# Input matrices of a state-space layer: powers turned once and read back by channel group, coefficients taken from a row layout

## The chip, the cores and the metric

The kernel is one program on one core of a Trainium2 chip. The metric is the device time of one execution in microseconds (us), smaller is better. The engines named are TensorE (PE; its weight loads are listed apart as PEld), VectorE (DVE), ScalarE (ACT), GpSimd (POOL) and SyncE (SP). SP and ACT each issue transfers on a DMA queue of their own (SPq, ACTq). Engines run their own lists of instructions in order and wait for one another through semaphores.

## What is computed

Two transformer blocks run one after the other on 512 tokens of width 1024, in float32. The first block has an attention layer with its MLP and a state-space layer with its MLP; the second is a modulated block with convolution, attention and a gated FFN. The change concerns matrices that the state-space layer needs and that depend on weights only:

```python
dt = jnp.exp(log_dt)[..., None]
a_bar = jnp.exp(lam * dt)                       # complex, per direction, group and state
b_bar = ((a_bar - 1.0) / lam)[..., None] * b_mat
bu = jnp.einsum('sgh,gph->sgp', u_row, b_bar[r])
...   # h_t = a_bar * h_(t-1) + bu_t, in both directions
return jnp.einsum('sgp,ghp->sgh', states, c_mat[r]).real
```

There are 64 groups of 16 channels, 64 states and 2 directions. The kernel cuts the 512 tokens into 64 chunks of 8. For that it needs, for each group, an "input matrix" that carries the 8 tokens x 16 channels of a chunk (128 rows) to the 2 directions x 64 states (128 columns), real and imaginary: each entry is a power of `a_bar` (by token in the chunk) times a coefficient of `b_mat` (by channel) times the gain of the norm. An "output matrix" and a "lag kernel" (what a token does to the others of its chunk) are built from the same powers.

## The kernel before

All weights come as units of 128 x 1024 numbers. A unit is loaded by SP into `raw`, rounded to the matmul's format by ACT (`hi`, L1115, tile `WH`), and DVE takes the rest of it (`lo`, L1643, tile `WL`). A product of two split operands is three matmuls (L444, L445, L446). SP loads a unit into a slot of `raw` when DVE is done with the one before (`unit_ready`).

The MLP of the first layer runs as 64 steps k = 0..63, each 24 matmuls of 128x512 on PE, in two halves of 32. Steps 0 to 15 of a half are up-projection tiles: ACT evicts each with L1328 and L1330, DVE splits it with L2056 (`AH`) and L2058 (`AL`). Steps 16 to 23 and 24 to 31 are the down-projection's two column halves; after step 23 and step 31 DVE adds four tiles of PSUM to `h` (L2072). Step 32, the first of the second half, uses PSUM banks that the evictions after step 31 free (`down_add`).

Beside the steps each engine calls `beside(k)`, an order that is written out by hand: the state-space matrices are built there, in 16 blocks b of 4 groups, block b around step `TURNS[b]`:

```python
TURNS = (9, 12, 17, 20, 24, 27, 30, 32, 35, 38, 41, 44, 49, 52, 57, 60)
```

The powers come first. DVE computes them in `beside(0)` to `beside(2)` (`powers`, `input_powers`) and, in `beside(4)`, the output powers (`output_powers`: L1810, L1814, L1815, tiles `pd` and `PC`). Then for each block, with T = TURNS[b]:

- ACT, step T-4: loads the block's coefficients with the states on partitions, `bc`.
- DVE, step T-2: `input_matrix(b)`: the gain into `bc` (L1827), four products of 512 per partition (L1829), a difference and a sum (L1833, L1835), into `WIp` with states on partitions.
- DVE, step T-1: `output_matrix(b)` (four of L1845, then L1850 and L1852).
- PE, after step T: `matrices(b)`: eight 128x128 transposes of `WIp` into PSUM (L558). ACT copies them to `WIe` (L1155) and stores it to `wi_scratch` (L1157).
- PE, after step T+1: `kernels(b)`: 16 small matmuls for the lag kernels (L573); ACT evicts them and stores the output matrix and, a step later, the kernels; DVE mends the middle lag (`lag_zero`, L1859, L1862) in step T+2.

The state-space layer after the MLP loads `wi_scratch` back (SP, L389). DVE comes to a step's `beside` after its share of the step's own work, so `beside(k)` on DVE runs after PE has ended step k, while PE is in step k+1.

## Time and profile before

| | |
|---|---|
| time, median of 3 runs | 1870.07 us (1869.59 to 1875.5) |
| profiled execution: its own time / its span | 1871.1 us / 1869.3 us |
| PE busy | 1788.6 us (96%) |
| DVE busy | 1298.9 us (69%) |
| ACT busy | 780.1 us (42%) |
| mean granted TensorE clock | 0.984 of full speed |
| moved by DMA | 224.98 MB, 120 GB/s |
| the chain that ended last | PE 89%, DVE 8%, ACT 1%, issue 1% |

The span is from the first to the last instruction; the time of the execution has 1.8 us around it. The chain that ended last is followed back from the last instruction to what released each step. A share of busy time is a mean over stages with different limits, so the stage of the change has to be read by itself: the first layer's MLP lies at about 300 to 660 us of the span.

### The profile page before, as it was taken

Reading aid. Unit: us, or ns where it says so; the run is one execution under the profiler, and the core shown is the slowest. Engines: PE = TensorE matmul, PEld = TensorE weight load, DVE = VectorE, ACT = ScalarE, POOL = GpSimd, SP = SyncE. Lnnn points to the kernel's source line nnn. Section 1 sums busy time; section 2 is a strip of 40 time slices with the busy share of each in tenths; the row PEclk is TensorE's granted clock in tenths of the full one; section 3 lists DMA queues with packets and bytes.
Section 4 is the critical chain, followed back from the end, with each engine's and each line's share of the span. In section 5 each row is a group of like instructions: output and inputs, shape, how many; then the busy total and the mean of one; then the engine's idle time right before and its main releaser. Section 6 shows DMA issues by size and latency. Waiting matters only on the chain.

```text
span 1869.3 us, 25467 instructions
## 1 busy us (share of the span) xinstructions
PE 1788.6 (96%) x9314; PEld 1439.4 (77%) x9314; DVE 1298.9 (69%) x2395; ACT 780.1 (42%) x1273; POOL 48.2 (3%) x39
## 2 busy tenths in 40 slices
PE   7999999999999992999999999999999999999998
PEld 6886688888888862888888788779755778888886
DVE  4868967767886669536655686448899976677465
ACT  5237954422342372424321332244687343333211
POOL 0000000000000000000000000000043100000000
PEclk9999999999999995999999999999999999999999
DMA  7320022444554489433444676224111223223532
GB/s 212 102 90 23 1 70 97 143 148 150 172 156 153 141 254 139 149 100 136 147 146 147 202 231 226 79 68 125 35 35 46 68 80 103 98 90 101 180 102 68
DMA packets 99927, 224.98 MB, mean 120 GB/s; under 512 B 19296, under 2 KB 48608, under 8 KB 99824
## 3 DMA queue, kind: packets, MB, share of 16 engines
q1 hardware_dynamic: 53520, 166.81, 28.8%
q10 hardware_dynamic: 46304, 56.77, 9.8%
q8 instruction: 67, 1.10, 0.2%
q14 instruction: 36, 0.29, 0.1%
HBM read 202.68 MB, written 20.87 MB: 120 GB/s over the span
## 4 chain that ended last, share of the span: by engine, by line
PE 89%; DVE 8%; ACT 1%; issue 1%; ACTq 0%; DVEq 0%
PE PS L444 26%; PE PS L445 26%; PE PS L446 26%; PE PS L634 2%; DVE ST L2125 1%; PE PS L1020 1%; PE PS L659 1%; PE PS L994 1%; DVE Sst L2129 1%; DVE Sst L2132 1%; PE PS L647 1%; PE PS L1028 1%; PE PS L558 1%; PE PS L504 1%; PE PS L1021 1%; PE PS L779 1%
## 5 line engine op out<-in xcount | busy, mean ns | idle before, releaser
L1643 DVE TENSOR_TENSOR WL<-raw,WH 128x1024 fp32r<-128x1024 f32 x228 | 279.7, 1232 | 275.9 <-ACT WH L1115 266.5
L1115 ACT CAST WH<-raw 128x1024 fp32r<-128x1024 f32 x228 | 237.3, 1046 | 489.5 <-PE PS L446 410.2
L444 PE MATMUL PS<-XH,WH 128*128 128x512 f32 x928 | 366.3, 395 | 4.5 <-DVE XL L1677 4.3
L446 PE MATMUL PS<-XH,WL 128*128 128x512 f32 x928 | 362.8, 391 | 0.0
L445 PE MATMUL PS<-XL,WH 128*128 128x512 f32 x928 | 362.6, 391 | 0.0
L444 PE MATMUL PS<-WH,AH 128*128 128x512 f32 x688 | 269.6, 392 | 0.0
L446 PE MATMUL PS<-WH,AL 128*128 128x512 f32 x688 | 267.9, 389 | 0.0
L445 PE MATMUL PS<-WL,AH 128*128 128x512 f32 x688 | 267.7, 389 | 0.0
L444 PE MATMUL PS<-WH,XH 128*128 128x512 f32 (+2 forms) x512 | 197.7, 386 | 11.6 <-DVE XL L1713 10.6
L444 PEld LDWEIGHTS PS<-XH,WH 128*128 128x128 f32 x928 | 175.0, 189 | 43.1 <-DVE XL L1677 4.9
L446 PEld LDWEIGHTS PS<-XH,WL 128*128 128x128 f32 x928 | 175.0, 189 | 37.2
L445 PEld LDWEIGHTS PS<-XL,WH 128*128 128x128 f32 x928 | 175.2, 189 | 34.9
L445 PE MATMUL PS<-WL,XH 128*128 128x512 f32 (+2 forms) x512 | 195.5, 382 | 0.0
L444 PEld LDWEIGHTS PS<-WH,AH 128*128 128x128 f32 x688 | 129.1, 188 | 28.8 <-issue 2.6
L446 PEld LDWEIGHTS PS<-WH,AL 128*128 128x128 f32 x688 | 129.1, 188 | 27.2
L445 PEld LDWEIGHTS PS<-WL,AH 128*128 128x128 f32 x688 | 129.2, 188 | 26.3
L446 PE MATMUL PS<-WH,XL 128*128 128x512 f32 (+2 forms) x384 | 145.7, 380 | 0.0
L1328 ACT ACTIVATE tmp<-PS 128x512 f32<-128x512 f32 x64 | 38.3, 598 | 197.4 <-PE PS L446 197.4
L444 PEld LDWEIGHTS PS<-WH,XH 128*128 128x128 f32 x512 | 96.8, 189 | 30.9 <-issue 11.2
L445 PEld LDWEIGHTS PS<-WL,XH 128*128 128x128 f32 x512 | 96.9, 189 | 17.4 <-issue 0.2
L1608 ACT ACTIVATE F<-PS,fb,fw 128x512 f32<-128x512 f32 x44 | 34.3, 780 | 142.9 <-PE PS L446 142.9
L2056 DVE CAST AH<-tmp 128x512 fp32r<-128x512 f32 x64 | 27.2, 425 | 83.1 <-ACT tmp L1330 82.6
(369 smaller groups left out, 2465.8 us busy)
## 6 DMA issues: line engine op xcount, KB each, us to landing
raw<-units_dram SPq DMA_DIRECT2D x272, 512.0 KB, 3.3
ada_late<-ada_units_dram ACTq DMA_DIRECT2D x48, 512.0 KB, 4.3
wi_scratch<-WIe ACTq DMA_DIRECT2D x16, 512.0 KB, 2.9
ca_scratch<-CAr ACTq DMA_DIRECT2D x32, 256.0 KB, 3.5
WI<-wi_scratch SPq DMA_DIRECT2D x16, 512.0 KB, 8.8
CA<-ca_scratch SPq DMA_DIRECT2D x16, 512.0 KB, 7.0
Tm<-k_scratch SPq DMA_DIRECT2D x8, 512.0 KB, 18.4
bc<-bc_dram ACTq DMA_DIRECT2D x16, 160.0 KB, 2.2
```

The source lines that it names most:

```text
L444: pe.matmul(o, lh, rh, start=start, stop=False)
L445: pe.matmul(o, lh, rl, start=False, stop=False)
L446: return pe.matmul(o, ll, rh, start=False, stop=stop)
L504: m = pe.transpose(turned_columns(ts, k, t, bank), h[:, t, k * P:(k + 1) * P], ident[:, :])
L558: m = pe.transpose(PS[:, bank0(k) + n // 4, (n % 4) * P:(n % 4 + 1) * P], WIp[:, n % 2, n // 2].rearrange("p j h -> p (j h)"), ident[:, :])
L634: m = pe.matmul(psum(2 * (n % 2) + c), QT[r, hh, t * P:(t + 1) * P], KT[r, hh, :], start=True, stop=True)
L647: m = pe.transpose(psum(4 + i % 2)[:, kt * P:(kt + 1) * P], Am[:, i % 2, kt * P:(kt + 1) * P], ident[:, :])
L1115: nc.scalar.copy(WH[:, (u + n) % SLOTS], raw[:, s]).then_inc(hi_done, 1)
L1328: nc.scalar.activation(tmp[:, f % 2, :], psum(4 + f if layer and first and f < 2 else f % 4), ACT.Relu).then_inc(up_relu, 1)
L1608: nc.scalar.activation(F[:, half, q, :], psum(up2_bank(f, first)), ACT.Identity, scale=fw[:, bass.ds(n, 1), 1], bias=fb[:, bass.ds(n, 1)]) ...
L1643: v.tensor_tensor(WL[:, s], raw[:, (u + n) % 2], WH[:, s].bitcast(F32), ALU.subtract).then_inc(unit_ready, 1)
L2056: v.tensor_copy(AH[:, f, :], tmp[:, 2 + f % 2, :]).then_inc(up_hi, 1)
```

## The change

The input matrix is built with tokens and channels on partitions from the start, the way it is stored. The powers (`PWI`, 128 x 8 x 128) are transposed once, after step 5 (8 transposes), and written to DRAM (`p_scratch`). For each block ACT then loads `PT`, the turned powers, each row of 8 tokens repeated to 16 channels, and `BT`, coefficients from a new input `bt` whose 16 channel rows are repeated for 8 tokens. DVE multiplies `PT` by `BT` and by the gain (now a scalar per partition, `gain_t`) in eight instructions of 256 instead of four of 512, and adds and subtracts into `WIe`, which is stored at once. `matrices(b)` and its eviction are gone, `output_powers` moves from `beside(4)` to `beside(3)`, and its end is signalled to PE (`w_done`). The gain is still multiplied into `bc`, since the lag kernels use it.

```diff
+        p_dram = nc.dram_tensor("p_scratch", [CHUNK, NG, 2, P], F32).ap()
...
-                def matrices(b):
+                def powers_turned():
+
+                    pe.wait_ge(w_done, 1)
+                    for j in range(CHUNK):
+                        m = pe.transpose(PS[:, 4 + j // 4, (j % 4) * P:(j % 4 + 1) * P], PWI[:, j].rearrange("p r g -> p (r g)"), ident[:, :])
+                    m.then_inc(m_turned, 1)
...
-                    pe.wait_ge(w_done, 2 * b + 2)
+                    pe.wait_ge(ca_done, 2 * b + 2)
                     if k // 8 % 4 == 2:
                         pe.wait_ge(up_relu, 16 * (k // 32 + 1))
                     if k // 8 % 4 == 3:
                         pe.wait_ge(down_add, 8 * (k // 32) + 4)
-                    if b:
-                        pe.wait_ge(ev_wi, b)
-                    for n in range(2 * BG):
-                        m = pe.transpose(PS[:, bank0(k) + n // 4, (n % 4) * P:(n % 4 + 1) * P],
-                                         WIp[:, n % 2, n // 2].rearrange("p j h -> p (j h)"), ident[:, :])
-                    m.then_inc(m_turned, 1)
...
-                        elif k in TURNS:
-                            matrices(TURNS.index(k))
+                        elif k == 5:
+                            powers_turned()
...
-                def evict_wi(b):
-
-                    bank = 0 if TURNS[b] // 8 % 4 == 2 else 4
-                    a.wait_ge(m_turned, b + 1)
-                    if b:
-                        a.wait_ge(wi_stored, 16 * b)
-                    nc.scalar.copy(WIe[:, :], PS[:, bank:bank + 2, :].rearrange("p a n -> p (a n)")).then_inc(ev_wi, 1)
-                    a.wait_ge(ev_wi, b + 1)
-                    a.dma_start(wi_dram[b], WIe[:, :]).then_inc(wi_stored, 16)
+                def evict_powers():
+
+                    a.wait_ge(m_turned, 1)
+                    nc.scalar.copy(WIe[:, :, :, :].rearrange("p g r q -> p (g r q)"), PS[:, 4:6, :].rearrange("p a n -> p (a n)")).then_inc(ev_wi, 1)
+                    a.wait_ge(ev_wi, 1)
+                    for r in range(2):
+                        a.dma_start(p_dram[:, :, r, :].rearrange("j g q -> g j q"),
+                                    WIe[64 * r:64 * r + 64].rearrange("g a r q -> g (a r) q")).then_inc(wi_stored, 16)
+
+                def pb_load(b):
+
+                    pairs = lambda x: x[:, :, :, :].rearrange("p g r q -> p (g r q)")
+                    sh = [CHUNK, SG, 2 * BG * P]
+                    a.dma_start(pairs(PT), p_dram[:, BG * b:BG * (b + 1)].rearrange("j g r q -> j (g r q)").unsqueeze(1).to_broadcast(sh)).then_inc(pb_in, 16)
+                    a.dma_start(pairs(BT), io["bt"][b].unsqueeze(0).to_broadcast(sh)).then_inc(pb_in, 16)
+
+                def store_wi(b):
+
+                    a.wait_ge(w_done, 2 * b + 3)
+                    a.dma_start(wi_dram[b], WIe[:, :, :, :].rearrange("p g r q -> p (g r q)")).then_inc(wi_stored, 16)
+                    if b < NB - 1:
+                        pb_load(b + 1)
...
-                        if k in TURNS:
-                            evict_wi(TURNS.index(k))
+                        if k == 5:
+                            evict_powers()
+                        if k == 6:
+                            a.wait_ge(wi_stored, 32)
+                            pb_load(0)
+                        if k + 1 in TURNS:
+                            store_wi(TURNS.index(k + 1))
...
-                        order.after(v.tensor_tensor(PC[64:P, :, ri, :][:, ::-1], pd[64:P, 2 * ri], pd[64:P, 2 * ri + 1], op))
+                        m = v.tensor_tensor(PC[64:P, :, ri, :][:, ::-1], pd[64:P, 2 * ri], pd[64:P, 2 * ri + 1], op)
+                        if ri == 0:
+                            order.after(m)
+                            order.wait()
+                    m.then_inc(w_done, 1)
                     order.wait()
+                    v.wait_ge(w_done, 1)
...
-                    for n, (i, j) in enumerate(((0, 0), (1, 1), (0, 1), (1, 0))):
-                        v.tensor_tensor(Dp[:, n, :, 0:CHUNK], x[i], y[j], ALU.mult).then_inc(d_prod, 1)
...
+                    v.wait_ge(pb_in, pb_in_base + 32 * b + 32)
+                    for n in range(2):
+                        for g in range(BG):
+                            y = BT[:, g] if n == 0 else BT[:, g, ::-1]
+                            v.scalar_tensor_tensor(out=DpT[:, n, g], in0=PT[:, g], scalar=gain_t[:, BG * b + g:BG * b + g + 1], in1=y,
+                                                   op0=ALU.mult, op1=ALU.mult).then_inc(d_prod, 1)
+                    v.wait_ge(wi_stored, 32 + 16 * b)
+                    for n, op in enumerate((ALU.subtract, ALU.add)):
+                        v.wait_ge(d_prod, 12 * b + 4 + 4 * n)
+                        v.tensor_tensor(WIe[:, :, n], DpT[:, n, :, 0], DpT[:, n, :, 1], op).then_inc(w_done, 1)
...
-                        if k == 4:
+                        if k == 3:
                             output_powers()
```

Three places of the order that the two programs give their engines follow. The first is DVE's list around steps 3 and 4, before and then after. L2056 and L2058 (L2080 and L2082 in the changed kernel) are a step's split, L1643 (L1664) is its weight unit, and L1810 to L1815 (L1831 to L1836) are the output powers.

```order
L2056 CAST AH<-tmp 128x512 [waits up_sq]
L2058 TENSOR_TENSOR AL<-tmp,AH 128x512 [waits up_hi]
L1643 TENSOR_TENSOR WL<-raw,WH 128x1024 [waits hi_done]
L1810 TENSOR_TENSOR pd<-Ak,pt 128x576 x4
L1814 TENSOR_TENSOR PC<-pd 64x9x64 [waits dve_order]
L1815 TENSOR_TENSOR PC<-pd 64x9x64
L1814 TENSOR_TENSOR PC<-pd 64x9x64
L1815 TENSOR_TENSOR PC<-pd 64x9x64
```

```order
L2080 CAST AH<-tmp 128x512 [waits up_sq,dve_order]
L2082 TENSOR_TENSOR AL<-tmp,AH 128x512 [waits up_hi]
L1664 TENSOR_TENSOR WL<-raw,WH 128x1024 [waits hi_done]
L1831 TENSOR_TENSOR pd<-Ak,pt 128x576 x4
L1835 TENSOR_TENSOR PC<-pd 64x9x64 [waits dve_order]
L1836 TENSOR_TENSOR PC<-pd 64x9x64
L1835 TENSOR_TENSOR PC<-pd 64x9x64 [waits dve_order]
L1836 TENSOR_TENSOR PC<-pd 64x9x64
L2080 CAST AH<-tmp 128x512 [waits up_sq,w_done,dve_order]
```

Before, the output powers follow the unit of step 4; now they follow that of step 3, and the split of step 4 comes behind them. The second place is PE's list of the changed kernel where step 5 ends and step 6 begins (L449 to L451 are L444 to L446 of before); nothing stood between the two steps before.

```order
L451 MATMUL PS<-XH,WL 128x512
L556 MATMUL PS<-ident,PWI 128x128 [waits w_done]
L556 MATMUL PS<-ident,PWI 128x128 x7
L449 MATMUL PS<-XH,WH 128x512 [waits unit_ready,up_relu]
```

The eight transposes wait for `w_done`, which the last of the output powers raises. The third place is ACT's list in steps 28 to 30 (blocks 5, 6 and 7), before and then after.

```order
L1115 CAST WH<-raw 128x1024 [waits unit_used,unit_in0]
L1184 DMA bc<-bc_dram 128x320 [waits k_done]
L1166 COPY Ke<-PS 128x112 [waits k_stored1,k_done]
L1167 COPY Ke<-PS 128x112
L1172 DMA ca_scratch<-CAr 512x1x128 [waits ca_done]
L1172 DMA ca_scratch<-CAr 512x1x128
L1115 CAST WH<-raw 128x1024 [waits unit_used,unit_in1]
L1178 DMA k_scratch<-Ke 128x240 [waits k_mid,ev_k]
L1115 CAST WH<-raw 128x1024 [waits unit_used,unit_in0]
L1155 COPY WIe<-PS 128x1024 [waits wi_stored,m_turned]
L1157 DMA wi_scratch<-WIe 128x1024 [waits ev_wi]
```

```order
L1187 DMA ca_scratch<-CAr 512x1x128
L1117 CAST WH<-raw 128x1024 [waits unit_used,unit_in1]
L1170 DMA wi_scratch<-WIe 128x1024 [waits w_done]
L1164 DMA PT<-p_scratch 128x1x1024
L1165 DMA BT<-bt_dram 128x1x1024
L1193 DMA k_scratch<-Ke 128x240 [waits k_mid,ev_k]
L1117 CAST WH<-raw 128x1024 [waits unit_used,unit_in0]
L1117 CAST WH<-raw 128x1024 [waits unit_used,unit_in1]
L1199 DMA bc<-bc_dram 128x320 [waits k_done]
L1170 DMA wi_scratch<-WIe 128x1024 [waits w_done]
L1164 DMA PT<-p_scratch 128x1x1024
L1165 DMA BT<-bt_dram 128x1x1024
```

In step 29 ACT now issues the store of block 6 and the two loads of block 7; in step 30 the copy and the store are gone.

## Rows read from the trace of the kernel before

**Rows 1.** The page: the span.
```profile
span 1869.3 us, 25467 instructions
```

**Rows 2.** Stretches: us; PE, PEld, DVE, ACT, POOL busy; granted clock; DMA share; GB/s.
```profile
300.00:660.00 360.00, 359.81 (x2107) 292.92 (x2106) 263.02 (x418) 127.79 (x189) 0.00 (x0) 1.00 0.49 152
664.00:670.00 6.00, 5.85 (x65) 4.99 (x63) 1.97 (x6) 4.26 (x8) 0.00 (x0) 1.00 1.00 386
```

**Rows 3.** PE in order of time around block 0's transposes: start, us.
```profile
343.85 0.39 PE L446 MATMUL PS<-XH,WL 128*128 128x512 f32 x1
344.09 1.03 PE L558 MATMUL PS<-ident,WIp 128*128 128x128 f32 x8
...
345.19 0.40 PE L445 MATMUL PS<-XL,WH 128*128 128x512 f32 x1
```

**Rows 4.** PE and DVE in order of time, end of step 5 and output powers.
```profile
322.09 0.39 PE L446 MATMUL PS<-XH,WL 128*128 128x512 f32 x1
322.32 0.39 PE L444 MATMUL PS<-XH,WH 128*128 128x512 f32 x1
...
319.59 0.42 DVE L2056 CAST AH<-tmp 128x512 fp32r<-128x512 f32 x1
321.79 2.76 DVE L1810 TENSOR_TENSOR pd<-Ak,pt 128x576 f32<-128x576 f32 x4
326.93 0.76 DVE L1815 TENSOR_TENSOR PC<-pd 64x576 f32<-64x576 f32 x1
```

**Rows 5.** ACT, DVE and PE in order of time, steps 29 to 32.
```profile
463.54 1.05 ACT L1115 CAST WH<-raw 128x1024 fp32r<-128x1024 f32 x1 [4.83 <-PE PS L446]
...
471.58 2.50 DVE L1829 TENSOR_TENSOR Dp<-PWI,bc 128x512 f32<-128x512 f32 x4
...
476.00 0.50 PE L444 MATMUL PS<-XH,WH 128*128 128x512 f32 x1 [0.19 <-DVE h L2072]
```

**Rows 6.** DVE, groups of 300 to 660 us: busy, mean ns.
```profile
L1829 DVE TENSOR_TENSOR Dp<-PWI,bc 128x512 f32<-128x512 f32 x64 | 40.0, 686 | 0.6
L1733 DVE TENSOR_TENSOR pw<-Ak 128x256 f32<-128x256 f32 x4 | 1.7, 424 | 0.1
```

**Rows 7.** DMA issues by line: KB each, median us to landing.
```profile
wi_scratch<-WIe ACTq DMA_DIRECT2D x16, 512.0 KB, 2.9
WI<-wi_scratch SPq DMA_DIRECT2D x16, 512.0 KB, 8.8
Tm<-k_scratch SPq DMA_DIRECT2D x8, 512.0 KB, 18.4
Cx<-ctx_dram ACTq DMA_DIRECT2D x2, 512.0 KB, 6.0
```

**Rows 8.** ACT, DVE and PE around blocks 0 and 1: times that give the slack.
```profile
340.01 1.04 ACT L1115 CAST WH<-raw 128x1024 fp32r<-128x1024 f32 x1
347.43 0.34 ACTq L1157 DMA_DIRECT2D wi_scratch<-WIe  x1
354.44 2.50 DVE L1829 TENSOR_TENSOR Dp<-PWI,bc 128x512 f32<-128x512 f32 x4
346.38 0.75 DVE L1852 SCALAR_TENSOR_TENSOR CAr<-Dp 128x576 f32<-128x576 f32 x1
350.51 0.66 PE L573 MATMUL PS<-CAr,bc 64*16 64x128 f32 x32
```

**Rows 9.** Stretches with sparse PE work, and two matmuls at the lower clock.
```profile
1218.00:1224.00 6.00, 5.50 (x15) 4.44 (x16) 3.19 (x7) 1.50 (x3) 0.00 (x0) 0.50 0.00 0
1212.00:1218.00 6.00, 1.48 (x10) 0.84 (x8) 3.12 (x13) 4.58 (x8) 0.00 (x0) 0.98 0.00 0
149.40:160.00 10.60, 7.21 (x40) 3.59 (x38) 9.34 (x17) 8.06 (x18) 0.00 (x0) 1.00 0.00 0
...
1219.94 0.63 PE L444 MATMUL PS<-XH,WH 128*128 128x512 f32 x1
1220.37 0.63 PE L445 MATMUL PS<-XL,WH 128*128 128x512 f32 x1
```

More of the change, by code:

```diff
@@ L84 @@
 INPUTS = ("x_in x_t units ada_units c_cols ident rope_cos rope_sin rope2_cos rope2_sin norm_mix_col norm_ffn_col "
-          "q_gain k_gain lam_vecs subln_col a_re a_im log_dt bc d_col d_gain lag_mask "
+          "q_gain k_gain lam_vecs subln_col a_re a_im log_dt bc bt gain_t d_col d_gain lag_mask "
           "b_ada_col b_ada_row ctx conv_w conv_b conv_ln_g conv_ln_b q_norm_col kv_norm_col b_o ln1_g ln1_b "
@@ L170, in program @@
         pd = at("pd", 16 * KB, [P, 4, CHUNK + 1, NG])
-        WIp = at("WIp", 16 * KB, [P, 2, BG, CHUNK, SG])
-        WIe = at("WIe", 20 * KB, [P, 2 * BG * P])
+        PT = at("PT", S0, [P, BG, 2, P])
+        BT = at("BT", 16 * KB, [P, BG, 2, P])
+        DpT = at("DpT", S0 + 9 * KB, [P, 2, BG, 2, P])
+        WIe = at("WIe", 20 * KB, [P, BG, 2, P])
+        gain_t = at("gain_t", small + 5888, [P, NG])
         Ke = at("Ke", 24 * KB, [P, 2, LAGS, SG])
@@ L247, in program @@
         consts_in = sem("consts_in")
-        x_in = sem("x_in_sem")
+        x_in = sem("x_in_and_pb_in")
         mod_out = sem("mod_out")
@@ L545, in bank0, with kernels @@
                     return 0 if k // 8 % 4 == 2 else 4
-                def matrices(b):
+                def powers_turned():
[3 more added lines that the diff above has]
+                    m.then_inc(m_turned, 1)
+                def kernels(b):
                     k = TURNS[b]
-                    pe.wait_ge(w_done, 2 * b + 2)
+                    pe.wait_ge(ca_done, 2 * b + 2)
                     if k // 8 % 4 == 2:
@@ L554, in matrices @@
                         pe.wait_ge(down_add, 8 * (k // 32) + 4)
-                    if b:
-                        pe.wait_ge(ev_wi, b)
-                    for n in range(2 * BG):
-                        m = pe.transpose(PS[:, bank0(k) + n // 4, (n % 4) * P:(n % 4 + 1) * P],
-                                         WIp[:, n % 2, n // 2].rearrange("p j h -> p (j h)"), ident[:, :])
-                    m.then_inc(m_turned, 1)
-                def kernels(b):
-                    pe.wait_ge(ca_done, 2 * b + 2)
                     if b:
@@ L1261, in _ @@
                     load(pt[64 * r:64 * r + 64, 2, :], io["log_dt"][r].partition_broadcast(64), ssm_in)
+                load(gain_t[:, :], io["gain_t"], ssm_in)
                 entry_hi(t_o, lambda k: subln[:, 1:2], 0, range(2, KD))
-                a.wait_ge(ssm_in, 16 * 4)
+                a.wait_ge(ssm_in, 16 * 5)
                 nc.scalar.activation(pt[:, 3, :], pt[:, 2, :], ACT.Exp).then_inc(sp_act, 1)
@@ L1737, in rates @@
                 def rates():
-                    v.wait_ge(ssm_in, 16 * 4)
+                    v.wait_ge(ssm_in, 16 * 5)
                     v.wait_ge(sp_act, 1)
@@ L1814, in output_powers @@
                         order.after(v.tensor_tensor(PC[0:64, :, ri, :], pd[0:64, 2 * ri], pd[0:64, 2 * ri + 1], op))
-                        order.after(v.tensor_tensor(PC[64:P, :, ri, :][:, ::-1], pd[64:P, 2 * ri], pd[64:P, 2 * ri + 1], op))
+                        m = v.tensor_tensor(PC[64:P, :, ri, :][:, ::-1], pd[64:P, 2 * ri], pd[64:P, 2 * ri + 1], op)
[3 more added lines that the diff above has]
+                    m.then_inc(w_done, 1)
                     order.wait()
+                    v.wait_ge(w_done, 1)
                 def input_matrix(b):
-                    gs = slice(b * BG, (b + 1) * BG)
-                    sh = [P, BG, CHUNK, SG]
-                    x = [PWI[:, :, ri, gs].rearrange("p m g -> p g m").unsqueeze(3).to_broadcast(sh) for ri in range(2)]
-                    y = [bc[:, b % 2, ri].unsqueeze(2).to_broadcast(sh) for ri in range(2)]
                     v.wait_ge(bc_in[b % 2], 16 * (b // 2 + 1))
@@ L2555, in host_layout @@
             np.tile(f(z["norm_mix"])[1].reshape(1, NB, BG, SG), (P, 1, 1, 1))], 1).transpose(2, 0, 1, 3, 4),
+        "bt": np.stack([f(z[n])[0].transpose(0, 2, 1, 3).reshape(P, NB, BG, SG) for n in ("ssm_b_re", "ssm_b_im")]).transpose(2, 4, 3, 0, 1).reshape(NB, SG, 2 * BG * P),
+        "gain_t": np.tile(f(z["norm_mix"])[1].reshape(NG, SG).T, (CHUNK, 1)),
         "d_col": by_group(f(z["ssm_d"])[0]), "d_gain": by_group(f(z["norm_mix"])[1]),
```

19 lines of the change are left out of this document (7 added, 12 removed).

## The prediction

> **What bounds the kernel now.** I read the stretches first. In the MLP of the first layer, where all of the change lies, PE is busy 359.81 of 360 us at the full clock, DVE 263.0 and ACT 127.8 [rows 2]. The reader is to see that PE sets the time of this stage, that ACT is far from a limit, and that DVE, at 73% as a mean, can be one in places. So an instruction less on PE is worth its slot, unless PE then waits for DVE. To find such places I read the engines in order of time: around a block of transposes [rows 3], where the moved output powers meet PE [rows 4], and between steps 29 and 32 [rows 5]. In the last, PE starts step 32 at 476.00 and has waited 0.19 us for DVE's L2072. It is the one step of the stage with no slack on DVE. Everything after the stage hangs on its end, so a change there shifts what follows by the same amount; the page gives a span of 1869.3 us [rows 1], the execution took 1871.1.
>
> **The transposes removed.** Two neighbouring matmuls of a step start 0.23 us apart (322.09 and 322.32) [rows 4]. Around a block, the last matmul of the step starts at 343.85 and the second of the next step at 345.19: 1.34 us where two periods would be 0.46 [rows 3]. A block costs PE 0.88 us. Sixteen go and one is added after step 5, so 15 net. The one after step 30 can't be collected, since DVE sets the start of step 32 (below). That leaves 14 x 0.88 = 12.3 us. The copies L1155 that go are on ACT, busy 127.8 of 360 us [rows 2], and are worth nothing.
>
> **The output powers moved, and a new wait on PE.** In DVE's list of before, step 3's weight unit is followed by the split of step 4 at 319.59; the output powers run from 321.79 to 326.93 + 0.76 = 327.69, which is 5.90 us [rows 4]. In the new order they start at 319.59 and end at 325.49. PE, however, is now told to wait for that end right after step 5, and its next instruction would start at 322.32 [rows 4]. With 0.06 us for the semaphore (my allowance) PE stands still for 325.55 - 322.32 = 3.2 us. Queued behind it is all of step 6, so this is lost whole. What covers DVE's move before is gone: in the old order nothing on PE asked for the output powers before step 10. The term could be smaller only if DVE reached the powers earlier, and it does not, because the split and unit of step 3 ahead of them are unchanged; ends 3.1 to 3.5. ACT waits there too, for the transposes it must copy, but has nothing due before PE ends step 6.
>
> **The products on DVE.** Four products of 512 start 0.605 us apart ((2.50 - 0.686) / 3) [rows 5, 6]. An instruction of 256 takes 0.262 us less than one of 512 (0.424 against 0.686) [rows 6], so 0.343 apart; eight make 2.74 against 2.42, 0.3 us more per block. It is a different instruction, of tensors with a scalar; L1852, which is of that kind, takes 0.75 us for 576, no more than its neighbours [rows 8], so I take no extra. Ends: 0 (the smaller ones cost only their elements) and 1.0 us. At 15 blocks it lies in DVE's idle time. At block 7, in step 30, it is on the path: L1829 starts at 471.58 and the chain from there through L1835 and L2072 leads to PE at 476.00 [rows 5]. Cost 0.3 us.
>
> **The loads.** Each block now brings 512 KB of `PT` and 512 KB of `BT` on ACT's queue, right after its 512 KB store. Usually they are issued two or more steps ahead. Block 1 as the pattern: ACT is free at 341.05 [rows 8], issues three times 0.34, the last from 341.7, and DVE wants the data at 354.44 less the 0.88 that PE saves in between [rows 8], so there is room for a landing of 11.8 us. Ten of the 15 gaps are two steps, four longer. One is a single step: the loads of block 7 go out in step 29 and are wanted in step 30. There ACT is free at 463.54 + 1.05 = 464.6 [rows 5] (block 6's product is ready at about 463.8), so the last load goes out at 465.3, and 471.58 leaves room for 6.3 us. No row shows such a load. A lone 512 KB store lands in 2.9 us, two loads of 512 KB in a row on ACT's queue in 6.0, loads in a burst of eight in 8.8 [rows 7]. So the wait lies between 0 and 2.5 us. The nearest row is the pair at 6.0; here it is the third in a row, and one transfer more is 0.524 MB at the 386 GB/s of a full DMA stretch [rows 2], 1.4 us: landing 7.4, wait 1.1 us. DVE waits, behind it stand L2072's evictions, and PE waits for those. The pause of PE at that place grows from 0.19 to about 2.5 us. The first loads (step 6, wanted in step 7) may also be late by some tenths; there PE has 2.2 us of slack before it needs the block's lag kernels, so I count none.
>
> **The sum.** 12.3 - 3.2 - 0.3 - 1.1 = 7.7 us less. Against the profiled execution 1871.1 - 7.7 = 1863.4; it is 1.0 above the median of the three runs, so against that 1870.07 - 7.7 = 1862.4. The extra input `gain_t` is one small load ahead of a wait that is covered, and the 17 MB of added traffic meet a DMA share of 0.49 [rows 2]; both are taken as nothing.
>
> **Rivals.**
>
> The loads move at half rate. Their sources have the eight tokens as outermost dimension, one of them with no stride. If that confines a load to half of the DMA engines, it moves at 193 GB/s: 1.05 MB take 5.4 us, the store's half share ahead 1.4, the fixed part of the store's 2.9 us is 1.5 (2.9 - 1.4), so both have landed 8.3 us after PT's issue at 464.95, at 473.3, or 474.6 with a weight unit between. The wait becomes 1.7 to 3.1, the gain 5.7 to 7.1, the time about 1863.7. Against it: no row shows any load at half rate. Chance 0.25. The Trainium skill, in "DMA: Bandwidth & Descriptors", section "Rules for kernel authors", states that an outermost dimension smaller than 16, such as a leading zero-stride broadcast, confines the DMA to at most that many engines. By that rule the wait would be the long one; no row of this case shows such a transfer, so the trace neither agrees nor disagrees.
>
> The clock falls. PE now stands idle for 3 us after step 5 and some 2.5 us before step 32. Where PE was busy only 1.48 of 6 us the granted clock went to 0.50 in the next stretch; where it was busy 7.21 of 10.6 with shorter gaps it stayed at 1.00 [rows 9]. At the lower clock, 1.2 GHz, matmuls start 0.43 us apart instead of 0.23 (1219.94, 1220.37) [rows 9], so 6 us of it cost 2.8 us and 3 us cost 1.4. One fall gives 7.7 less 1.4 to 2.8, 4.9 to 6.3 us of gain, about 1864.5. Chance 0.20.
>
> PE waits for DVE in more places, because with 0.88 us less per block and 0.3 more work DVE's slack shrinks. Block 0's output matrix ends at 347.13 and PE asks for it at 350.51 [rows 8], a slack of 3.4, of which 2.2 are left. So this would need DVE to be about 2 us slower than counted at ten blocks or more. It would end inside 0.3% of before, 1865 to 1870. Chance 0.10.
>
> Slower: the loads land late at every gap. The price decides from a landing of 11.8 + 2.2 = 14.0 us: beyond that each of the ten two-step gaps stalls PE by the excess. Block 7 then waits 14.0 - 6.3 = 7.7 us, which with the 3.5 of the other terms leaves 1.1 of the 12.3, so a tenth of a us more at the ten gaps turns the sign. The one row that lies there is the `Tm` load at 18.4 us [rows 7], which moves its 512 KB in pieces of 128 numbers and in a burst of eight; it would make 10 x 4.4 + 12.1 + 3.5 - 12.3 = 47 us more, 1917. `PT` and `BT` move rows of 1024 numbers. Chance 0.05.
>
> More than forecast: DVE's chain at step 32 or the wait after step 5 is shorter than I read, gain above 9.5 us. Chance 0.05.
>
> **How the numbers follow.** The forecast as summed has 0.35, the most of one case, and gives the time, 1862.4. Its own range is 1861 to 1864. The range for 8 in 10 takes in the half-rate loads and most of the falls of the clock, and on the other side the smaller ends of the wait and the products (12.3 - 3.1 = 9.2, 1860.9) and part of the last case: 1859 to 1867. About 0.3%, 5.6 us, is what a measurement of this kernel can tell from no change, so faster means below 1864.5. Faster: 0.35 + 0.21 of the half rate + 0.06 of the clock + 0.04 = 0.66. Slower: 0.05 and a little for what I don't see, 0.06. The same: the rest, 0.28.
>
> **What would show it.** After step 5 an idle PE of 3.2 us before eight transposes, released by DVE. No transposes at steps 9 to 60, and a step's last matmul and the next step's first 0.23 us apart there. At the start of step 32 an idle PE of 1.4 us plus DVE's wait for the loads; the time to landing of `PT` and `BT` against 7.4 us says which of the first two cases holds. Eight products of about 0.42 us each, 2.8 us in all. The granted clock at 1.00 in the slices around 325 and 475 us. Wrong would be: no idle PE after step 5, which would mean that DVE is earlier there than its order says; or idle times of PE before the small lag matmuls, which would mean that DVE has become the limit.

## The result

The changed kernel takes 1912.16 us (median of 4 runs, 1910.95 to 1915.16), the kernel before 1870.36 beside it: ratio 1.0206, 95% interval 1.0191 to 1.022. It is 2.1% slower; the forecast was 1862.4 with a range to 1867. No case but the fourth rival, "slower", with a chance of 0.05, had a time above that of before.

The page of the profile after, its span and its chain of work that ended last:

```profile
span 1909.1 us, 25307 instructions
...
PE 56%; DVE 13%; DMA 10%; ACT 2%; issue 2%; ACTq 0%; DVEq 0%; SPq 0%
PE PS L449 17%; PE PS L451 16%; PE PS L450 16%; DMA raw<-units_dram 5%; DMA BT<-bt_dram 4%; DVE DpT L1854 2%; DVE WL L1664 2%; DVE ST L2149 1%; PE PS L1022 1%; PE PS L996 1%; DVE Sst L2156 1%; DVE Sst L2153 1%; DVE WIe L1859 1%; PE PS L1030
```

Transfers hold 10% of the chain, the weight units and `BT`. Three stretches after: the stage, and two within PE's pause ahead of step 32 (columns as in [rows 2]):

```profile
300.00:660.00 360.00, 315.56 (x1759) 253.50 (x1758) 243.75 (x429) 99.68 (x148) 0.00 (x0) 0.96 0.65 179
494.00:496.00 2.00, 0.00 (x0) 0.00 (x0) 0.00 (x0) 0.33 (x1) 0.00 (x0) 0.50 0.50 147
500.00:503.00 3.00, 0.00 (x0) 0.00 (x0) 3.00 (x8) 0.00 (x0) 0.00 (x0) 0.50 0.00 0
```

PE's 359.81 busy us of [rows 2] are 315.56 now. From 494 to 496, with the pair and the last of a weight unit in flight, DVE and PE wait for data and the DMA engines are 0.50 busy as a mean of the sixteen, at 147 GB/s, as if half of them worked. From 500 to 503 DVE is at its products alone and PE stands by at the lower clock, 1.2 GHz. The waits after between 300 and 720 us, of PE, DVE and ACT (us in total, times, longest):

```profile
PE PS L575 <- DVE CAr L1876: 16.6, 9, 3.8
PE PS L449 <- DVE h L2096: 14.2, 1, 14.2
PE PS L449 <- DVE WL L1664: 5.9, 4, 1.7
PE PS L575 <- DVE Ke L1886: 4.9, 1, 4.9
PE PS L556 <- DVE PC L1836: 3.1, 1, 3.1
...
DVE WL L1664 <- ACT WH L1117: 79.0, 16, 7.2
...
DVE DpT L1854 <- DMA BT<-bt_dram: 15.9, 5, 8.4
DVE CAr L1874 <- issue: 8.1, 1, 8.1
...
ACT WH L1117 <- DMA raw<-units_dram: 128.6, 27, 11.4
```

Read it from below. ACT waits 128.6 us for weight units (before 2.3 us, 4 times); DVE waits 79.0 us for ACT's halves of them, and 15.9 us for `BT`; PE waits 44.7 us in all for DVE, where before it waited 0.2 [rows 5]. Only the last sum is time lost. ACT and DVE had idle time before too, but PE set it: ACT waited 228.3 us for PE's matmuls and DVE 53.1 us for ACT's halves, and PE stood still for neither. After, it is the transfers that ACT waits for, and the lateness reaches PE. Around step 32, DVE in order of time:

```profile
490.20 0.28 DVE L1849 TENSOR_TENSOR bc<-bc 128x128 f32<-128x128 f32 x1
498.87 3.25 DVE L1854 SCALAR_TENSOR_TENSOR DpT<-PT,gain_t,BT 128x256 f32<-128x256 f32 x8 [8.39 <-DMA BT<-bt_dram]
502.04 1.29 DVE L1859 TENSOR_TENSOR WIe<-DpT 128x512 f32<-128x512 f32 x2
503.25 2.72 DVE L2096 SCALAR_TENSOR_TENSOR h<-PS,ss,h 128x512 f32<-128x512 f32 x4
```

Of the same step, the chain that ended last. Each pair of loads can be issued only when the products have read the pair before:

```profile
464.24 14.87 DMA BT<-bt_dram
...
484.69 14.08 DMA BT<-bt_dram
...
502.12 1.22 DVE WIe L1859 x2
...
504.36 0.62 ACTq L1165
```

One turn of that loop is 484.69 - 464.24 = 20.5 us. Three steps of the stage, the usual distance of two blocks, are some 16.3 us (3 x 5.44, a step being 24 matmuls 0.227 us apart). So the pairs fall behind wherever nothing gives them more.

The stage ends (start of the last update of `h`) at 704.77, before at 666.00, 38.8 us later. The terms: 15 blocks of transposes less, 13.2 us; 44.5 us more of waiting; what is left, 38.8 + 13.2 - 44.5 = 7.5 us, is found by subtraction. The clock accounts for most of it: in four stretches between 357.7 and 583.0 PE is busy 13.7 us at a granted clock of 0.50, and with matmuls 0.43 us apart in place of 0.23 [rows 9] that is 6.4 us (an estimate). After the stage's end both kernels need the same (1204.3 and 1203.3 us).

### The profile page after: what moved, and what is told of

Same layout as the page of the kernel before. It is cut to its first block, busy times and chain, and to the rows that moved or that the text cites. A ratio compares the mean times of both kernels' runs of the same rounds, so it can differ in the third digit from the quotient of the medians.

```text
span 1909.1 us, 25307 instructions
## 1 busy us (share of the span) xinstructions
PE 1783.5 (93%) x9194; PEld 1431.6 (75%) x9194; DVE 1309.6 (69%) x2459; ACT 766.9 (40%) x1258; POOL 48.2 (3%) x39
## 4 chain that ended last, share of the span: by engine, by line
PE 56%; DVE 13%; DMA 10%; ACT 2%; issue 2%; ACTq 0%; DVEq 0%; SPq 0%
PE PS L449 17%; PE PS L451 16%; PE PS L450 16%; DMA raw<-units_dram 5%; DMA BT<-bt_dram 4%; DVE DpT L1854 2%; DVE WL L1664 2%; DVE ST L2149 1%; PE PS L1022 1%; PE PS L996 1%; DVE Sst L2156 1%; DVE Sst L2153 1%; DVE WIe L1859 1%; PE PS L1030 1%; PE PS L1023 1%
## 5 line engine op out<-in xcount | busy, mean ns | idle before, releaser
L1664 DVE TENSOR_TENSOR WL<-raw,WH 128x1024 fp32r<-128x1024 f32 x228 | 279.4, 1231 | 302.2 <-ACT WH L1117 291.7
L449 PE MATMUL PS<-XH,WH 128*128 128x512 f32 x928 | 368.4, 397 | 18.3 <-DVE h L2096 14.2
L451 PE MATMUL PS<-XH,WL 128*128 128x512 f32 x928 | 364.7, 393 | 0.0
L449 PE MATMUL PS<-WH,AH 128*128 128x512 f32 x688 | 269.1, 391 | 5.9 <-DVE WL L1664 5.9
L451 PE MATMUL PS<-WH,AL 128*128 128x512 f32 x688 | 267.7, 389 | 0.0
L449 PEld LDWEIGHTS PS<-XH,WH 128*128 128x128 f32 x928 | 176.8, 191 | 57.7 <-DVE h L2096 14.5
L449 PE MATMUL PS<-WH,XH 128*128 128x512 f32 (+2 forms) x512 | 197.6, 386 | 11.3 <-DVE XL L1734 10.4
L451 PEld LDWEIGHTS PS<-XH,WL 128*128 128x128 f32 x928 | 176.6, 190 | 37.3
L449 PEld LDWEIGHTS PS<-WH,AH 128*128 128x128 f32 x688 | 129.1, 188 | 36.5 <-issue 10.0
L451 PEld LDWEIGHTS PS<-WH,AL 128*128 128x128 f32 x688 | 129.2, 188 | 26.8
L451 PE MATMUL PS<-WH,XL 128*128 128x512 f32 (+2 forms) x384 | 145.7, 379 | 0.0
L449 PEld LDWEIGHTS PS<-WH,XH 128*128 128x128 f32 x512 | 96.8, 189 | 30.2 <-issue 11.0
L2022 DVE SCALAR_TENSOR_TENSOR mod_acc<-ada_late,c_act,mod_acc 128x512 f32<-128x512 f32 x112 | 81.4, 747 | 2.0
```

What stands on the lines that cost most here:

```text
L449: pe.matmul(o, lh, rh, start=start, stop=False)
L451: return pe.matmul(o, ll, rh, start=False, stop=stop)
L1664: v.tensor_tensor(WL[:, s], raw[:, (u + n) % 2], WH[:, s].bitcast(F32), ALU.subtract).then_inc(unit_ready, 1)
L2022: v.scalar_tensor_tensor(out=acc, in0=w, scalar=c, in1=acc, op0=ALU.mult, op1=ALU.add).then_inc(mod_sum, 1)
```

## The experiments

All ratios are to executions of the kernel before taken beside each run; their medians lie between 1870.36 and 1873.48 us, so a ratio does not follow from a run's time and the 1870.36 above. Landings are from issue to the end of the data, medians. Idle PE is summed over 300 to 720 us, by what on DVE it waited for: the update of `h` before step 32, the output matrix (`CAr`) or the middle lag (`Ke`) before lag kernels, the output powers after step 5, and a step's weights (`WL`); other waits, 2.1 us at most, are left out. Landings, idle times and stage ends come from one profiled execution of each kernel; that of e1_rows_gap38 took 1877.06 us, the longest of its 11 and 5.7 us above their median.

| run | ratio (95%) | PT, BT land | idle PE: step 32 / CAr / Ke / powers / WL | stage end |
|---|---|---|---|---|
| before | 1 | | 0.2 | 666.0 |
| after | 1.0206 (1.0191 to 1.0220) | in the chain 11.3 to 14.9 | 14.2 / 16.6 / 4.9 / 3.1 / 5.9 | 704.8 |
| a3_lead8 | 1.0200 (1.0164 to 1.0236) | | 14.6 / 13.8 / 5.4 / 3.1 / 3.9 | 701.8 |
| a2_rows128 | 0.9970 (0.9958 to 0.9983) | 5.1, 5.9 | 1.8 / 0 / 2.1 / 3.2 / 0 | 661.0 |
| c1_distinct_lead16 | 0.9990 (0.9977 to 1.0004) | 5.5, 7.4 | 3.1 / 0 / 2.6 / 3.2 / 0 | 661.9 |
| a4_lead16 | 1.0056 (1.0036 to 1.0075) | 8.4, 11.1 | 12.6 / 2.0 / 2.8 / 3.1 / 0 | 677.4 |
| b1_lead16_early | 1.0040 (1.0028 to 1.0053) | 8.4, 11.0 | 12.7 / 2.0 / 3.3 / 0 / 0 | 672.9 |
| c2_one_load | 0.9992 (0.9980 to 1.0004) | | 1.9 / 3.8 / 0 / 3.2 / 0 | 664.9 |
| d1_unread | 1.0156 (1.0127 to 1.0185) | | 5.8 / 12.8 / 6.7 / 3.1 / 1.9 | 694.4 |
| a1_bt_rows | 1.0039 (1.0028 to 1.0050) | | 9.4 / 2.4 / 2.1 / 3.1 / 0 | 671.6 |
| c3_spaced | 1.0007 (0.9996 to 1.0019) | 8.4, 10.8 | 1.1 / 7.1 / 0 / 0 / 4.2 | 665.8 |
| c4_spaced_rows | 0.9959 (0.9945 to 0.9972) | 8.3, 9.4 | 0 / 0.6 / 0 / 0 / 4.2 | 658.4 |
| d3_before_spaced | 1.0032 (1.0016 to 1.0047) | | 0 / 0 / 0 / 0 / 4.2 | 670.5 |
| d4_rows_early | 0.9995 (0.9986 to 1.0005) | 8.3, 9.3 | 10.7 / 0 / 1.0 / 0 / 0 | 665.6 |
| e1_rows_gap38 | 0.9986 (0.9975 to 0.9997) | 8.2, 9.3 | 0 / 0 / 11.0 / 0 / 0 | 665.3 |
| e2_before_gap38 | 0.9997 (0.9986 to 1.0008) | | 0 | 664.6 |
| e3_after_gap38 | 1.0191 (1.0176 to 1.0207) | | 1.1 / 10.2 / 19.4 / 3.1 / 3.1 | 698.0 |

The theories: E, an outermost dimension of 8 confines the loads to half of the engines; R, reading the same rows again and again is slow; V, the added bytes are too many.

**128 plain rows** (a2_rows128). Both loads read 128 rows that the host wrote out.

```diff
-a.dma_start(pairs(BT), io["bt"][b].unsqueeze(0).to_broadcast(sh))
+a.dma_start(pairs(BT), io["bt_rows"][b])              # PT: io["bt_rows"][(b + 1) % NB]
```

> The two loads of each block are taken from 128 rows written out in DRAM (leading dimension 128, no row twice); the values of PT are replaced by coefficients of another block, so the output matrices of the state-space layer are not computed. Volume, queue and places are those of the changed kernel. Theory E (a load whose source has a leading dimension of 8 uses only half of the DMA engines): the loads land like other 512 KB transfers, PT and BT within 5 to 7.5 us of issue, DVE's products start unhindered at all places but block 7, and the time is 1860 to 1866. Theory R (the same rows read 8 or 16 times are slow): the same, 1860 to 1866. Theory V (17 MB more on the DMA engines beside the weights is what hurts): no better than the changed kernel, 1905 to 1915.

1869.03 us, 0.997. The same 17 MB at a higher rate, 203 GB/s over the stage where after has 179, and the loss is gone: V falls. Block 7's pair had landed at 471.33, 5.9 us after the issue of `BT` (465.46), within the 6.3 us that the prediction had found there.

**Leading 8, no repeats** (a3_lead8). Each row stands 8 times in DRAM with a skipped row between groups, so that the load keeps 8 outermost.

```diff
+a.dma_start(pairs(BT), io["bt_rows"][b][:, 0:SG])     # [8, 16+1, n]
```

> As the run before, 128 different rows, but with a leading dimension of 8 (each eighth is followed by one row of padding, so that the source is 8 x 16 rows); PT's values are again replaced. Theory E: as slow as the changed kernel, 1905 to 1915, BT lands 11 to 15 us after its issue. Theory R: fast, 1860 to 1866. Theory V: 1905 to 1915.

1911.19 us, 1.020, ACT's wait for weights again above 100 us:

```profile
ACT WH L1117 <- DMA raw<-units_dram: 122.4, 27, 10.4
```

No row is read twice here, and the loss is all there (two executions, 1908.22 and 1914.16 us). V fell above, and R has nothing to act on here; E is left.

**Sixteen outermost** (a4_lead16). Rows in channel-major order, so that 16 stands outside and 8 inside; the store turns them back. Full computation.

```diff
-sh = [CHUNK, SG, 2 * BG * P]
+sh = [SG, CHUNK, 2 * BG * P]
-io["bt"][b].unsqueeze(0).to_broadcast(sh)
+io["bt"][b].unsqueeze(1).to_broadcast(sh)
...
-a.dma_start(wi_dram[b], ...)
+a.dma_start(wi_dram[b].rearrange("(j h) n -> h j n", h=SG), ...)
```

> The rows on the partitions are ordered by channel and then by token, so that the sources are 16 x 8 rows with rows still repeated 8 or 16 times; the store puts them back in the old order. The whole computation is done. Theory E: fast, with all 16 DMA engines: sum of the prediction with the products at their measured 0.75 us more: 12.3 - 3.2 - 0.75 - 0 to 2.5 of waiting at block 7 = 6 to 8 us faster than before, 1862 to 1865. Theory R: as slow as the changed kernel, 1905 to 1915. Theory V: 1905 to 1915.

1882.45 us, 1.0056: three quarters of the loss back, but neither expectation. `PT` and `BT` land in 8.4 and 11.1 us, not in 5.1 and 5.9.

**The early signal** (b1_lead16_early). PE waits for the powers alone; ACT's copy waits for the output powers.

```diff
-step(v.tensor_scalar(A8[:, 1, :, 1, :], ai, -1.0, None, ALU.mult))
+v.tensor_scalar(A8[:, 1, :, 1, :], ai, -1.0, None, ALU.mult).then_inc(w_done, 1)
+v.wait_ge(w_done, 1)
...
+a.wait_ge(w_done, 2)                                  # ACT, before its copy
```

> As the run before, and PE's eight transposes after step 5 wait only for the powers (end of DVE's step 2), not for the output powers; ACT's copy waits for those. If the 3.1 us that PE stood still after step 5 in the changed kernel are a loss of their own, this is 3.1 us faster than the run before, 1859 to 1862. Rival: DVE's moved work comes due later all the same and PE waits elsewhere in steps 6 to 12, less than 1 us faster.

1880.78 us, 1.004. The idle 3.1 us of PE after step 5 are gone. What that gives back is less sure: the two profiled spans are 3.2 us apart (1879.1 against 1882.3), the medians 1.7, and the intervals of the two ratios overlap. The expected 1859 to 1862 had a fast kernel as its start.

**Sixteen outermost, no repeats** (c1_distinct_lead16). As a3_lead8, with 16 groups of 8 rows.

```diff
+a.dma_start(pairs(BT), io["bt_rows"][b][:, 0:8])      # [16, 8+1, n]
```

> Same bytes and same 128 rows as in the run with 128 plain rows (ratio 0.997, BT lands 5.9 us after its issue), but each load now has two levels outside its rows, 16 x 8, with a skipped row between the sixteens, so that they can't be merged; no row is read twice. Both loads distinct, so the values of PT are not the powers and the outputs are not the reference's. Theory 'two levels': a 16 x 8 source is slow by its form, as in the kernel with repeated rows and 16 outermost (ratio 1.0056, landings 8.4 and 11.1 us): landings of 8 us or more, ratio 1.003 to 1.007. Theory 'repeats': reading the same DRAM rows eight or sixteen times is what slowed that kernel beside the plain rows: here landings of 5 to 6 us and a ratio of 0.996 to 0.999. If it is the latter, the outermost 16 is also enough for the full rate.

1868.94 us, 0.999; landings 5.5 and 7.4, the second later than the 5 to 6 us expected. So 16 outermost takes the loss away. Beside a4_lead16 its loads land 2.9 and 3.7 us earlier, but that is not yet R. The two runs differ in more than the repeats: a4_lead16 also stores `WIe` in another order right ahead of the pair, which is issued in 0.56 us and lands in 4.2, where the plain store takes 0.33 and 3.0. Block 0's pair has no store ahead of it. Issue (ns) and landing of `BT` for blocks 0 and 1, in a4_lead16, then here, then for block 1 of c4_spaced_rows below, where `BT` comes from plain rows behind the reordered store:

```profile
L1165 ACTq DMA_DIRECT2D BT<-bt_dram x1: 622/622/622, 335.5 to 335.5; - x1
DMA to landing us min/median/max: 6.4/6.4/6.4
...
L1165 ACTq DMA_DIRECT2D BT<-bt_dram x1: 1338/1338/1338, 349.3 to 349.3; - x1
DMA to landing us min/median/max: 10.7/10.7/10.7
...
L1165 ACTq DMA_DIRECT2D BT<-bt_rows_dram x1: 622/622/622, 334.6 to 334.6; - x1
DMA to landing us min/median/max: 6.2/6.2/6.2
...
L1165 ACTq DMA_DIRECT2D BT<-bt_rows_dram x1: 617/617/617, 347.9 to 347.9; - x1
DMA to landing us min/median/max: 7.0/7.0/7.0
...
L1166 ACTq DMA_DIRECT2D BT<-bt_rows_dram x1: 1585/1585/1585, 345.5 to 345.5; - x1
DMA to landing us min/median/max: 9.1/9.1/9.1
```

Without a store ahead, repeated and distinct rows land alike (`BT` 6.4 and 6.2 us, `PT` 4.7 in both); behind the reordered store even plain rows of `BT` are issued slowly and land late (`PT` between them still has its repeats). So R is not shown, and these rows speak for the store, alone or together with the repeats. No run changes the store alone.

**One pair of loads** (c2_one_load). Blocks from 1 on take block 0's tiles.

```diff
-                    if b < NB - 1:
-                        pb_load(b + 1)
```

> The changed kernel with the two loads of block 0 alone; all later blocks take that block's PT and BT, so the outputs are wrong from block 1 on. It leaves out 30 of the 32 loads and nothing else. Theory 'the loads are the loss': the terms of the prediction are left without the wait: 12.3 - 3.2 and, with the products at 0.75 us more in block 7, 8.3 us less than before, ratio 0.9955 to 0.997; the idle PE at step 32 is at most 1.5 us and ACT's wait for raw weights is back at about 8 us from 128.6. Rival 'the products or the reordering on DVE cost too': ratio 0.998 or more with PE waiting for DVE in several places.

1871.36 us, 0.9992: the ratio of the rival (0.998 or more), the reason of neither expectation. ACT's wait for weights is 4.1 us, so the loads are the loss beside after; but of the forecast gain nothing is there. The waits and three stretches show where it is (columns as above):

```profile
PE PS L575 <- DVE CAr L1874: 3.8, 1, 3.8
PE PS L556 <- DVE PC L1834: 3.2, 1, 3.2
PE PS L449 <- DVE h L2094: 1.9, 1, 1.9
...
324.00:328.00 4.00, 3.34 (x12) 3.05 (x13) 3.84 (x7) 1.01 (x1) 0.00 (x0) 0.57 0.00 0
358.00:362.00 4.00, 3.72 (x39) 2.76 (x40) 3.93 (x7) 1.01 (x3) 0.00 (x0) 0.58 0.41 85
481.00:484.00 3.00, 2.51 (x6) 2.02 (x7) 3.00 (x5) 0.41 (x2) 0.00 (x0) 0.59 0.89 289
```

Block 0's loads are late by 5.5 us for DVE and stop PE for 3.8 at its first lag kernels. After each of the three pauses the granted clock falls to 0.50 for some 3.5 us. The stage ends 1.1 us earlier than before: 13.2 less 3.2, 3.8 and 1.7 of more waiting leaves 4.5, and the 3.4 that are missing are put down to the three falls, which is not measured by itself (three times 3.4 us at the lower clock cost 4.7 us at most, by the same estimate as above).

**Loads that nobody reads** (d1_unread). All loads as after, but from block 1 on DVE neither waits for them nor reads them.

```diff
-v.wait_ge(pb_in, pb_in_base + 32 * b + 32)
+v.wait_ge(pb_in, pb_in_base + 32)
+a.wait_ge(pb_in, pb_in_base + 32 * b + 32)            # new, on ACT, before it issues the next pair
+yt, xt = (BT, PT) if b == 0 else (xs, xs)             # xs: a view of PC
```

> The changed kernel with all its loads (8 outermost), but from block 1 on nobody on DVE waits for them or reads them: the products take the output powers PC in place of PT and BT, so the outputs are not the reference's. ACT asks, before it issues a pair, for the landing of the pair before (one or more steps old). Theory 'direct wait' (PE loses its time because DVE waits for BT): what is left is the kernel with one pair of loads, ratio 0.999 to 1.002, though weights land late. Theory 'late weights' (the loads fill eight engines, the weight units have pieces there too, ACT and DVE then get the weights late): ACT's wait for raw stays above 100 us (128.6 after the change, 4 with one pair), PE still waits at steps 32 and others, ratio 1.012 or more.

1902.92 us, 1.0156, three quarters of the loss. ACT still waits 121.2 us for weights. So three quarters of the loss are there without any wait of DVE for `BT` after block 0, and late weights are one way by which they reach PE. It is not clean: the run gives ACT a wait of its own for the pair before, 36.8 us (7 times), so the share of the weights is at most these three quarters and is not shown apart from that wait.

**BT alone from plain rows** (a1_bt_rows). Full computation.

> The changed kernel with BT alone read from 128 plain rows; PT keeps 8 outermost. Full computation. Both loads in the slow form give a ratio of 1.0206, none (128 rows) gives 0.997. If the loss goes by the bytes that are confined to eight engines, half of it remains: 1.007 to 1.011. If it is a threshold (landings that pass the 11.8 us of a two-step gap), PT's 512 KB alone stay under it, and the ratio is 0.998 to 1.003, with waits at step 10 and step 32 only.

1880.86 us, 1.0039. Between the two expectations: with half of the confined bytes, 0.0069 of the 0.0236 between 0.997 and 1.0206 are left, three tenths. ACT still waits 86.1 us for weights, but PE feels it in few places.

**The blocks' steps moved** (c3_spaced, c4_spaced_rows, and the control d3_before_spaced).

```diff
-TURNS = (9, 12, 17, 20, 24, 27, 30, 32, 35, 38, 41, 44, 49, 52, 57, 60)
+TURNS = (9, 12, 17, 20, 24, 27, 30, 33, 36, 39, 42, 45, 49, 52, 57, 60)
```

> The kernel with 16 outermost and the early signal (ratio 1.0040, idle PE at step 32 12.7 us), with the blocks from the eighth on moved by one step each (33, 36, 39, 42, 45 in place of 32, 35, 38, 41, 44), so that no two blocks are less than three steps apart; full computation. Theory 'the single-step gap': the loads of block 7 have a second step, 10.5 us more, the 12.7 us at step 32 go whole, and the stage ends 12 us earlier: ratio 0.997 to 0.999. Rival 'late everywhere': with landings of 11 us beside a two-step gap of 11.8 us the idle time only moves to other steps, and less than 6 us come back: ratio 1.001 or more.

> As the spaced kernel, and BT is read from 128 rows laid out in DRAM by the host in the order of the partitions, with no repeats; PT still reads its rows sixteen outermost with repeats. Full computation. Theory 'form of the load': BT lands in 6 to 8 us in place of 11, weight units are less delayed, and with neither the idle time after step 5 nor that at step 32 it is the fastest of all: ratio 0.994 to 0.996, 12.3 - 0.8 = 11.5 us less at most. Rival: the stage ends earlier but what follows waits for its own transfers, as it did with the plain rows, where 5.0 us at the stage's end left 2.2 us of the span: ratio 0.997 to 0.999.

> The kernel before, with nothing changed but the blocks from the eighth on moved by one step each. It is the control for the kernel with spaced blocks and plain BT rows (ratio 0.9959, 8.9 us less). If the spacing by itself gives something, its ratio is under 0.999 and the gain of the turned form is smaller by that. I expect none: PE waits 0.2 us for DVE at step 32 in the kernel before, so there is nothing to collect; 0.999 to 1.001.

1874.14 us (1.0007), 1864.31 us (0.9959) and 1878.49 us (1.0032). c3_spaced differs from b1_lead16_early in the steps alone. The 12.7 us at step 32 went but for 1.1, as the first expectation has it, but 7.1 us in eight small waits and 4.2 in another came instead, and the ratio lies between the two expectations. c4_spaced_rows has the expected ratio, with `BT` landing in 9.4 us and not in 6 to 8. The control is a miss: I expected no effect, and it is slower. All three kernels with a block at step 45 show it:

```profile
574.50 0.17 DVE L1862 TENSOR_TENSOR Ke<-Ke,PS 128x16 f32<-128x16 f32 x1
...
574.87 0.76 PE L444 MATMUL PS<-WH,AH 128*128 128x512 f32 x1 [4.17 <-DVE WL L1643]
```

This is the kernel before with spaced blocks. PE may take the banks of step 48 only when the lag kernels of the block at 45 are cleared, and DVE's last touch of them (`Ke`, 574.50 + 0.17) ends 0.2 us before PE starts. The profile names `WL`, but `Ke` came last. Against its control the turned form with plain `BT` rows is at 0.9959 / 1.0032 = 0.993, against the kernel before at 0.9959, 7.7 us less: the fastest of those that compute everything.

**Fast loads at the old steps** (d4_rows_early).

> The kernel with spaced blocks and plain BT rows, but with the blocks at their old steps: PT and the early signal as there. Full computation. It shows what the single-step gap costs when the loads land in 7 to 9 us: by the prediction's reckoning of 6.3 us of room, a wait of 1 to 3 us on DVE and 3 to 6 us of idle PE at step 32 with a fall of the clock of 1.6 us; ratio 0.998 to 1.000, against 0.9959 spaced. Rival: the gap no longer matters once the loads land within 8 us, ratio 0.995 to 0.997.

1872.64 us, 0.9995, as expected, but by larger waits: DVE waits 6.3 us for `BT` (expected 1 to 3) and PE 10.7 at step 32 (expected 3 to 6).

**The single-step gap put elsewhere** (e1_rows_gap38, e3_after_gap38, and the control e2_before_gap38).

```diff
+TURNS = (9, 12, 17, 20, 24, 27, 30, 33, 36, 38, 41, 44, 49, 52, 57, 60)
```

> As the kernel with plain BT rows, the early signal and spaced blocks (0.9959), but with block 9 at step 38 and the next ones at 41 and 44, so that the one single-step gap is now 36 to 38, between feature steps, and no block's lag kernels have to be cleared at the edge of step 48, where every kernel with a block at 45 shows 4.2 us of idle PE. Full computation. Theory 'place': what costs at a single-step gap is that at step 32 DVE's updates of h stand behind the products and PE behind those; at steps 36 to 38 PE has some us of slack to DVE, the late loads (9.3 us against 6.3 of room) are mostly covered, and the 4.2 us and a fall of the clock of 1.6 us are gone: ratio 0.992 to 0.995. Theory 'gap': DVE's 6.3 us of waiting there delays weights and PE as at step 32, ratio 0.998 or more.

> The kernel before with the same steps for its blocks as the run with the gap at 38: its control. With spaced blocks it was slower (1.0032, 4.2 us of idle PE at step 48 and a fall of the clock); here no block stands at 45, so that should be gone: 0.999 to 1.001. Should it be 1.003 again, the edge of step 48 is not the cause.

> The changed kernel (8 outermost in both loads) with the steps of the run with the gap at 38. Full computation. If the wait at step 32 (14.2 us of idle PE) is a matter of the place alone, it goes and with it the low clock after it: some 14 to 20 us less, ratio 1.010 to 1.013. If the loads are late at every gap whatever the steps, most of it comes back at other steps: ratio 1.016 or more.

1871.36 (0.9986), 1871.37 (0.9997) and 1906.28 us (1.0191). The control moved nothing, so the edge of step 48 was the cause of the 4.2 us. e3_after_gap38 is as "late at every gap" has it: the 14.2 us at step 32 went but for 1.1, and 19.4 stand at the new place. In e1_rows_gap38, with fast loads, DVE waits no more than 1.3 us for `BT`, and still PE stands for 11.0 at the new place. The ratio is in the range of "gap", but the wait of 6.3 us that was to make it is not there. ACT and DVE of e1_rows_gap38 show why:

```profile
512.14 1.59 ACTq L1166 DMA_DIRECT2D BT<-bt_rows_dram  x1
...
514.43 1.33 ACTq L1188 DMA_DIRECT2D ca_scratch<-CAr  x1
...
522.32 0.76 DVE L1876 TENSOR_TENSOR CAr<-Dp 128x576 f32<-128x576 f32 x1 [6.59 <-issue]
```

The store of `CAr` is issued right behind the pair in the same queue and is done at 522.2, 7.8 us later (median of the stage 3.8). In a single-step gap DVE wants to overwrite `CAr` one step after it was stored, waits 6.6 us for that store (the profile shows it as "issue"; that the store is what ended the wait follows from the times, 522.24 and 522.32, and from DVE's list, which waits for it there), and with it everything behind it on DVE. The same row stands in after (8.1 us, the store issued at 505.71 and done at 517.75), in e3_after_gap38 (9.8) and with plain rows (3.4).

## Why the prediction was wrong

**Failed: "So the wait lies between 0 and 2.5 us", landing 7.4.** After, block 7's pair landed 14.1 us after the issue of `BT` (484.69 to 498.77), and DVE waited 8.4. The bound came from rows of loads that use all engines ([rows 7], 6.0 for a pair, 8.8 in a burst); an access form that no row showed was priced as if it were one of them. With plain rows (a2_rows128) they price it well: 5.9 us, wait 0.

**Failed: the price of the half-rate rival.** The mechanism is shown (a3_lead8 against c1_distinct_lead16: the same bytes, distinct rows in both, 8 against 16 outermost, 1.020 against 0.999), and its chance was 0.25. But I gave it 1863.7, as if the pair and the store shared the engines with one weight unit, and counted one place only. What was left out: a weight unit that is spread over all engines is done only when the eight crowded ones are. That is argued; shown is that its median landing (300 to 680 us) went from 3.6 us to 5.9, ACT's wait from 2.3 us to 128.6, and d1_unread keeps three quarters of the loss though DVE waits for no pair after the first. "ACT is far from a limit" was true of its busy time and false of its queue: it executes in order, and each late unit holds back the activations behind it. The Trainium skill, "DMA: Bandwidth & Descriptors", section "Rules for kernel authors", says that an outermost dimension under 16 confines a DMA to at most that many engines; the traces agree (DMA share 0.50 from 494 to 496, and the loss gone with 16 in place of 8). What it does to other transfers they show beyond it. The 17 MB by themselves, taken as nothing, are near that: a2_rows128 moves them too and is at 0.997.

**Right in kind, mis-sized: the loads late at every gap.** The slower rival decided "from a landing of 14.0 us", named ten gaps and gave 1917 at 18.4; measured 1912, with 14.9 the longest landing that the chain shows. It was near by accident: for the gaps its mechanism gives 10 x 0.9 at most at that landing. The rest came by what it did not have: late weights, the store of `CAr` and the clock, not told apart in size.

**Failed: "The first loads may also be late by some tenths ... I count none".** `BT` of block 0 took 11.3 us from its issue at 334.77 and DVE waited 5.1; PE stopped 3.3 at the block's lag kernels (3.8 in c2_one_load), where I had seen 2.2 of slack.

**Failed: the chance and place of the clock's falls.** Counted as one fall at a chance of 0.20, given by a row with pauses in a longer stretch of work [rows 9]. In c2_one_load the granted clock went to 0.50 at each of three pauses, of 3.2, 3.8 and 1.9 us, and 3.4 us in all are put down to that. After the change itself, the pause behind step 5 had no fall, and that of 14.2 had a long one. With the 3.8 of the first loads, this took nearly all of the forecast gain where no other load was left: 7.2 of 7.7 us, and 0.9992.

**Failed by omission: the store of CAr.** The prediction listed who is queued behind the wait on DVE and not who is queued behind the loads on ACT's queue. At a single-step gap that store lands 7.8 us after its issue in e1_rows_gap38 and 12.0 after the change, where the medians of the stage are 3.8 and 3.7, and one step on DVE waits for it.

**Mis-sized: the products.** Eight take 3.25 us against the 2.50 of before [rows 5], 0.75 more and not 0.3; they start 0.396 us apart ((3.25 - 0.479) / 7) and not 0.343. The range went to 1.0.

**Right.** PE idle after step 5: 3.1 us (forecast 3.2); b1_lead16_early has no such pause, and 1.7 us less by the medians. The transposes: 0.88 us a block, 13.2 in all (the forecast has 12.3, since it takes the fifteenth to become a longer pause at step 32; here the pauses are counted whole); the stage ends of the kernels with fast loads close with it within about 1 us (a2_rows128: 13.2 less 3.2, 2.1 and 1.6 of waiting and one fall of the clock is 4.7 to 6.3, measured 5.0).

## What to carry to other kernels

Read the source pattern of a new load from the outside in: here 8 in place of 16 in its first dimension was the whole loss, with the same bytes. When a run changes a store as well as a load, compare a place where only the load is there, as block 0's pair. Price a transfer not only for who waits for it, but for every transfer that shares its engines and every issue that stands behind it on its queue; an engine with a low busy share can still be the one whose order makes the rest late. Where a term of the sum is a wait in a form that no row shows, its upper end is not the slowest ordinary row.
